# A new order for the matmuls between the block products and the second MLP matmul

## The reference

```python
def squared_relu_mlp(h, w1, w2):
    a = jax.nn.relu(h @ w1)          # 1024 -> 4096
    return (a * a) @ w2              # 4096 -> 1024

for i in range(2):
    h = h + mixer_i(rms_norm(h, g_mix_i))     # conv mixers, then chunked gating
    h = h + squared_relu_mlp(rms_norm(h, mlp_norm_g[i]), mlp_w1[i], mlp_w2[i])
return rms_norm(h, final_norm_g)
```

## Time and profile before

| | us |
|---|---|
| median of 3 runs | 2760.87 (2759.73 to 2763.11) |
| profiled execution, whole | 2759.75 |
| profiled execution, span of the slowest core (core 1) | 2757.6 |
| PE busy | 2572.1 |
| DVE, ACT, POOL busy | 1397.9, 1052.4, 832.9 |
| PE waiting for GpSimd before line 923, in all | 65.7 |

### The profile page before, as it was taken

The page is one execution under the profiler, slowest core; times in us unless marked ns, Lnnn a source line. Parts: engine busy times, 40 slices in busy tenths (PEclk is TensorE's granted clock), DMA queues, the critical chain, the costliest instruction groups (busy, mean ns, idle before and its releaser), DMA issues.

```text
span 2757.6 us, 40724 instructions; the slowest of 8 cores (2745.1 to 2757.6 us)
## 1 busy us (share of the span) xinstructions
PE 2572.1 (93%) x12952; PEld 1220.0 (44%) x12952; DVE 1397.9 (51%) x2269; ACT 1052.4 (38%) x1792; POOL 832.9 (30%) x1028
## 2 busy tenths in 40 slices
PE   1879999999999999999999999999999999999998
PEld 0434444444454444444445444444445444445443
DVE  1766435744556433664456533565335753357334
ACT  2232336434334324543434422553443333364223
POOL 1113442434311333243321322322431123314323
PEclk9999999999999999999999999999999999999999
DMA  6677786557654332246555223213436333312321
GB/s 142 176 168 188 168 179 150 123 107 163 188 184 132 111 113 92 55 111 193 181 195 181 94 100 115 85 51 143 142 132 209 120 104 114 112 39 106 112 86 77
DMA packets 121905, 361.33 MB, mean 131 GB/s; under 512 B 24416, under 2 KB 70496, under 8 KB 104672
## 3 DMA queue, kind: packets, MB, share of 16 engines
q1 hardware_dynamic: 73536, 230.67, 24.1%
q0 software_dynamic: 37072, 55.58, 13.2%
q10 hardware_dynamic: 11088, 72.49, 7.3%
HBM read 326.20 MB, written 88.08 MB: 150 GB/s over the span
## 4 chain that ended last, share of the span: by engine, by line
PE 84%; DVE 5%; DMA 4%; issue 3%; POOL 1%; ACT 1%; SPq 0%; DVEq 0%; ACTq 0%; POOLq 0%
PE bank L923 33%; PE bank L837 24%; PE bank L778 11%; PE bank L765 9%; DVE Z L438 3%; PE bank L906 2%; PE bank L605 2%; PE bank L1035 2%; PE bank L715 2%; DMA scr_s<-Z 1%; POOL Z L438 1%; DMA scr_a<-Z 1%; DMA Z<-ev_w_in 1%; ACT Z L822 1%; DVE Z L1155 1%
## 5 line engine op out<-in xcount | busy, mean ns | idle before, releaser
L923 PE MATMUL bank<-Z 128*128 128x512 bf16 x4096 | 921.2, 382 | 65.7 <-POOL Z L438 65.7
L438 POOL TENSOR_TENSOR Z<-Z 128x512 bf16<-128x512 f32 x512 | 529.9, 1048 | 830.9 <-ACT Z L822 454.9
L786 DVE TENSOR_TENSOR h<-bank,h 128x512 f32<-128x512 f32 x640 | 432.1, 689 | 488.0 <-PE bank L923 382.0
L923 PEld LDWEIGHTS bank<-Z 128*128 128x128 bf16 x4096 | 399.2, 98 | 555.0 <-issue 92.7
L438 DVE TENSOR_TENSOR Z<-bank,Z 128x512 f32<-128x512 f32 x336 | 232.1, 691 | 573.8 <-PE bank L837 561.5
L837 PE MATMUL bank<-Z 128*128 128x512 f16 x1792 | 436.8, 384 | 10.3 <-DVE Z L438 10.2
L765 PE MATMUL bank<-xnT,Z 128*128 128x512 f16 x1792 | 396.8, 380 | 13.3 <-DVE Z L1164 8.1
L844 ACT ACTIVATE Z<-bank 128x512 f32<-128x512 f32 x336 | 186.7, 588 | 531.2 <-PE bank L837 529.1
L822 ACT ACTIVATE Z<-Z 128x512 f32<-128x512 f32 x336 | 211.4, 630 | 422.9 <-DVE Z L438 422.8
L837 PE MATMUL bank<-xnT,Z 128*128 128x512 f16 x1344 | 328.7, 381 | 0.0
L837 PEld LDWEIGHTS bank<-Z 128*128 128x128 f16 x1792 | 177.0, 99 | 230.7 <-issue 26.6
(11 more groups left out here) (100 smaller groups left out, 1811.0 us busy)
## 6 DMA issues: line engine op xcount, KB each, us to landing
Z<-wcache SPq DMA_DIRECT2D x66, 1024.0 KB, 4.9
Z<-wcache SPq DMA_DIRECT2D x55, 896.0 KB, 4.5
wcache<-Z ACTq DMA_DIRECT2D x29, 1024.0 KB, 8.0
wcache<-Z SPq DMA_DIRECT2D x28, 896.0 KB, 7.5
Z<-w POOLq DMA_DIRECT2D x48, 512.0 KB, 6.1
Z<-wcache ACTq DMA_DIRECT2D x21, 1024.0 KB, 6.2
h<-x SPq DMA_DIRECT2D x32, 512.0 KB, 9.3
Z<-w POOLq DMA_DIRECT2D x16, 1024.0 KB, 12.2
```

What stands on the lines that cost most here:

```text
L438: P.op(eng, lambda e: e.tensor_tensor(out=out, in0=in0, in1=in1, op=op), reads=reads, writes=writes)
L786: small("dve", lambda e: e.tensor_tensor(out=h[:, tb, d * 512:(d + 1) * 512], in0=banks[b][:], in1=h[:, tb, d * 512:(d + 1) * 512], op=ALU ...
L923: r = e.matmul(banks[b][:], lhsT=lhs(kc, tb), rhs=where[slot].v[:, kc, :], start=start and x_ == 0, stop=stop and x_ == len(ks) - 1)
```

## The change

In the last job of each quarter (m = 3), the step `B` is split: m7 with its copy stays where it was (`B7`), and m6 with its copy (`B6`) now comes after `D4` and `D3` of job 2. After the job, groups (0,0) and (0,1) both take first the four column blocks 0, 1, 4, 5; then comes `D4` of job 3, then both groups take blocks 2 and 6, then `C` of job 3; groups (1,0) and (1,1) and `D3` follow as before. `D4` of job 3 thus comes before its `C`. The four groups take the blocks in the order 0, 1, 4, 5, 2, 6. For m < 3 the order is what it was.

```diff
-            def B(self):
+            def B7(self):
                 self.r = get_bank()
                 self.mm("m7", self.r, True, True)
                 self.s7 = self.snap(self.r)
+
+            def B6(self):
                 self.mm("m6", self.c, False, True)
                 self.s2 = self.snap(self.c)
...
-                    job.B()
+                    job.B7()
+                    if m < 3:
+                        job.B6()
                     if prev is not None:
                         prev.D4()
                         prev.D3()
+                    if m == 3:
+                        job.B6()
                     prev = job
...
-                head, rest = (0, 1, 2, 4, 5, 6), (3, 7)
+                head, rest = (0, 1, 4, 5, 2, 6), (3, 7)
                 bk = {}
 
-                def early(tb, d):
-                    bk[tb, d] = get_bank()
-                    part(p2[d], tb, bk[tb, d], head, True, False)
-
-                early(0, 0)
+                def early(tb, d, ks):
+                    first = (tb, d) not in bk
+                    if first:
+                        bk[tb, d] = get_bank()
+                    part(p2[d], tb, bk[tb, d], ks, first, False)
+
+                early(0, 0, head[0:4])
+                early(0, 1, head[0:4])
+                prev.D4()
+                early(0, 0, head[4:6])
+                early(0, 1, head[4:6])
                 prev.C()
-                early(0, 1)
-                prev.D4()
-                early(1, 0)
+                early(1, 0, head)
                 prev.D3()
-                early(1, 1)
+                early(1, 1, head)
```

## The result

The changed kernel takes 2673.97 us (median of 4 runs), before 2761.99 us (the three runs shown ahead and a fourth); the ratio is 0.9676, interval 0.9649 to 0.9703. Forecast were 2673 us.

A forecast was written before the change was run, and what follows sets the result against it. TensorE's stream and what holds it up bound the kernel; removing 71.1 us of waits and 16.3 us of clock falls from 2760.87 gives 2673.5, stated as 2673 us. Range 2662 to 2698.

The forecast's parts named there:

- The wait of 2.15 us per change: TensorE's wait for GpSimd before the first early group, 32 times: all removed, 71.1 us with modelled ends.
- The second cost: Matmul groups after the pause run at 1.2 GHz at 10 of 32 changes, 1.63 us each: 16 us saved.
- the signs: Profile after: GpSimd waits gone or below 5 us, period 51.9 us, TensorE busy about 16 us less, idle about 66 less.
- The cost of the new neighbours: At each reordered product or early group, inputs arrive in time: taken as 0, up to 1 us a change kept for A.
- Rival D: Second piece of w2 comes late at each change: 41 us more than before, 2802 us; chance 0.01.
- Rival A: Smaller wait at m3 of job 3 or the last parts: 16 to 32 us back, 2689 to 2705; chance 0.10.
- Rival B: Clock falls stay or move, not hanging on this pause: only 71 us won, 2690 us; chance 0.09.
- Rival C: In the MLPs, longer unbroken stretches lower the clock; two falls a period give 17 us more, 2778; chance 0.03.

The follow-up runs named there:

- m6_late_only: Changed kernel with the early groups whole in the old interleaving, so only m6 of job 3 stays late; ratio to before 0.984, median 2725.19 us.
- first_group_split: Changed kernel with m6 of job 3 late but only early group (0,0) split, the rest in the old interleaving; ratio to before 0.9749.
- longer_pause: Kernel before with m3 of job 2 ahead of its m4 at the last job; ratio to before 1.019, median 2816.98 us.
- two_short_pauses: Changed kernel with whole early groups, m4 of job 3 between (0,0) and (0,1), and m3 of job 3 right after m5; ratio to before 0.9929.
- m3_right_behind_m5: Changed kernel with m3 of job 3 directly behind m5 instead of behind early group (1,0); ratio to before 0.9797.
- changed_again: The changed kernel, unmodified, run once more in a later batch beside other experiments; ratio to before 0.9667.

## Why the prediction was right

The list of waits named a single kind of wait, one per change, and the timeline gave its chain: 3.87 us from m4 to the use of its square, with 0.86 us of cover. The prediction was a placing of known durations on a new order, and each placing can be held against the trace after. That forecast and median lie 1 us apart is partly luck: the executions behind the ratio lie between 2667 and 2676 us.

- The wait of 2.15 us per change: gone in all 32. m6_late_only and first_group_split have pauses of 1.33 and 0.42 us, and cost 32 times that over the changed kernel within 1 us (the second with the reserve that its batch had no run of the changed kernel). longer_pause, with 3.07, is 128.7 us over the changed kernel of its batch; 32 x 3.07 = 98.2, and 147 falls on 8 cores at 1.63 us make the other 30. So the time of a pause on TensorE passes to the end undiminished.
- The second cost, the falls of the clock: the mechanism held, the size was 16 forecast and 19.9 measured. At the changes the 16 stands: the clock record of core 1 has the ten falls that I had counted, and the mean of the cores, 9.75, makes 9.75 x 1.63 = 15.9. The rest lies outside the changes, where my sum had nothing and only the range allowed one or two falls: 75 falls on all cores before, 61 after. Whether these hang on the change stays open (74 with the longer pause, 50 to 72 in the other kernels).
- Of the signs, the period, the waits and the idle time (66 us less) came as forecast. For the busy time I had named 16 us, but my own sum leaves 87 - 66 = 21, since the 32 x 0.17 us of modelled ends count as busy; measured are 24.8, which leaves 19.4 for the clock.
- The cost of the new neighbours was put at nothing, and is nothing. Block 2 had 1.3 us to spare (1.5 by the row, from 1301.1 to 1302.58, before GpSimd's signal). For m3 of job 3 I had 0.25, and the experiment says 0.19. The last parts start 0.6 us after the square, of which some 0.15 is the signal: 0.45, as forecast.
- Rival D did not come: the weights' second piece, needed 3.4 us earlier, is not in the list of waits at all, as its landing 5.8 to 11.6 us after an issue some 20 us ahead said.
- Rival A did not come: no wait at line 837 beyond those of the MLPs' start, none for GpSimd. Rival B did not come: with the pauses the clock went from 0.986 to 0.993 and the falls at the changes from 78 to none, and two_short_pauses shows that it is the single long pause. Rival C, in which longer unbroken stretches bring the clock down, did not come: 1.00 over whole periods.

The sum was 87 us and the fall of the median 88. That the whole change was needed does not follow: half of it would have done.

## What to carry to other kernels

Where an in-order engine waits once per stage for a short chain on three others, measure the chain from the start of its first instruction to the first use of its result, and fill that distance with work that is ready: the wait goes whole as soon as the filling is longer, and more filling gives nothing. Split a consumer that reads old and new inputs, so that the old ones are read first. Count with a pause on TensorE not only its length: see in the rows after it whether they run at the lower clock, and if it can't be removed, try to split it: here two pauses of 1.33 and 1.11 us were cheaper than one of 2.2.

## What the runs showed of the hardware

In these kernels the falls of the granted clock went with the length of a single pause. The table gives the pause from start to start on TensorE, which comes 32 times per core, at how many of the 256 changes of the profiled execution the clock fell to the lower level, and the clock lost as a mean over the cores:

| kernel | pause, us | falls at 256 changes | mean clock | lost, us |
|---|---|---|---|---|
| changed | none | 0 | 0.9934 | 17.6 |
| first_group_split | 0.42 | 0 | 0.9935 | 17.4 |
| m3_right_behind_m5 | 1.11 | 0 | 0.9928 | 19.6 |
| m6_late_only | 1.33 | 0 | 0.9933 | 18.3 |
| two_short_pauses | 1.33 and 1.11 | 0 | 0.9936 | 17.5 |
| before | 2.2 | 78 | 0.9864 | 37.5 |
| longer_pause | 3.1 | 147 | 0.9801 | 55.6 |

Up to 1.33 us no change has a fall. I had expected the loss to begin there already. Between 1.33 and 2.2 us nothing was tried.

The list of waits is not the same on all cores. The slowest core of before waited 65.7 us, core 2 of the same execution 73.4:

```profile
PE bank L923 <- POOL Z L438: 73.4, 32, 2.7
```

This does not mean that the chain takes longer there: records are missing. On core 2 (and on core 4, with 73.1) the group behind the wait has five matmuls at every one of the 32 changes, where the program has six:

```profile
1328.17 1.24 PE L923 MATMUL bank<-Z 128*128 128x512 bf16 x5 [2.20 <-POOL Z L438]
```

The record of the first is missing, and its 0.22 us count as waiting, 32 x 0.22 = 7 of the 7.7 us. Before comparing the waits of two cores, compare their numbers of matmul records (12817 and 12952 here).

The prediction said that the trace of before does not show the peak-current limit of which the Trainium skill speaks ("TensorE: Matmul & The Clock Gate", section "Seeing it yourself"). A later execution of the changed kernel (changed_again) shows a clock of that size. The first two rows are core 4, the third is core 6 of the same die:

```profile
200.00:280.00 80.00, 79.24 (x347) 35.31 (x351) 45.04 (x71) 26.43 (x41) 26.00 (x34) 0.81 0.67 166
600.00:800.00 200.00, 198.99 (x1010) 96.84 (x1018) 97.02 (x148) 86.02 (x147) 72.45 (x94) 1.00 0.70 176
```

```profile
200.00:280.00 80.00, 77.28 (x406) 36.87 (x405) 50.75 (x82) 28.07 (x44) 32.00 (x39) 1.00 0.80 192
```

0.81 is 13/16, held in a stretch in which TensorE is busy for 79 of 80 us. Core 5 has it as well, while cores 6 and 7 of the same die and the four cores of the other die have 1.00 or 0.98 with the same work. Later, with TensorE busy for 199 of 200 us, core 4 has 1.00. The Trainium skill's rule has this clock right, but it gives it to the whole die and for as long as the load lasts, and the trace shows it on two cores of the die and for a part of the dense work only. What brings it, no run here shows.
